# Two of four dense gate blocks scattered into the DRAM matrix by adding transfers instead of one-hot products

## The chip, the cores and the metric

The kernel runs on one core of one Trainium2 chip. The metric is the device time in microseconds (us) of one execution; for before it is the median of three runs. "Faster" and "slower" below refer to that time.

## The reference, cut to what matters

One encoder block: a shared input projection feeds an SSD mixer and an HGRN2 mixer, an output projection follows, and then a PEER layer retrieves experts. The PEER layer is what changes hands here:

```python
q = (xt @ w_query).reshape(t, PEER_HEADS, 2, PEER_HALF)
s = jnp.einsum('thpd,hpnd->thpn', q, sub_keys)
s_top, i_top = lax.top_k(s, PEER_TOPK)
...
c_top, c_idx = lax.top_k(cand, PEER_TOPK)
expert = idx1 * PEER_KEYS + idx2
gate = jax.nn.softmax(c_top, axis=-1)
...
u = u_table[eb]
hid = gelu(einsum('td,thkd->thk', xb, u)) * gb
out = einsum('thk,thkd->td', hid, v_table[eb])
```

There are 1024 tokens, 8 heads, 16 experts per head and 16384 = 128 x 128 experts of width 1024, all in float32.

## The kernel before

Tokens stand in 8 blocks of 128. The program is a row of stages with a barrier of all engines between them: `input_norm`, `ssd`, `hgrn`, `mix_out`, `peer`.

**Two ways through the experts.** Token blocks 4 to 7 are handled by gathers: one row of `u_rows` and of `v_rows` per token, head and choice. Blocks 0 to 3 (512 tokens) are handled densely: every expert's product with every one of these tokens is computed, and multiplied by a gate matrix that is zero except where the token chose the expert. That matrix is `sel` in DRAM, 8 batches of 128 x 128 x 64 float32 (64 tokens each, 4.19 MB a batch), read back in the main loop by ACT's queue (`load_sel`).

**Routing.** A unit is one token block and one head. Matrix products (`query`, `score`) make the scores; then VectorE finds the 16 experts (`route_keys`, `route_pairs`, `route_experts`) and their gates (`route_gates`, for unit n inside the route of unit n + 1). The 32 units of blocks 0 to 3 are routed in `mix_out`, which also computes the output projection block by block; a list `HEADS_IN` names for each block b the up to three heads whose query, score and two routes go with it. Heads 0 to 7 of that list are the units 0 to 15 (blocks 0 and 1), and the three heads of an entry go through TensorE in an order written out by hand at the end of `mix_out`'s tensor part. GpSimd only scales Y there.

**Building `sel` (first part of `peer`, before the main loop).** For 128 groups of 4 tokens: VectorE compares a counter with the second and the first key (`hot_b`, `hot_a`, two operations of 128x512, L1815); GpSimd multiplies `hot_b` by the gate (L1535); TensorE multiplies `hot_a` by `hot_b` for each of the 4 tokens (L1620), which gives that token's 128 x 128 gates; ACT copies them to a stage in two halves (L1696, L1699); SP stores a stage of 2.1 MB when 16 groups have filled it (L1515). `hot_a`, `hot_b` and the result bank are double-buffered by `j % 2`: VectorE starts group j when the products of j - 2 are done. Two units of block 4 and 5 are routed on the way (`ROUTE_AT`), since the gathers of the main loop need them. The main loop starts when the last stage has landed.

**Start of `hgrn`.** ACT first copies a projection that an earlier stage left in Y (`first_out`, L786), then the gates, exponentials and weights of head 0 are made by ACT and VectorE in turn; TensorE begins with L763.

The loop that feeds TensorE in the building of `sel` is, word for word:

```python
                pe.wait_ge(hot_a_ready, j + 1)
                pe.wait_ge(hot_b_ready, j + 1)
                need(pe, staged, 2 * (j - 1))
                for q in range(4):
                    mm = nc.tensor.matmul(ps_o[:, j % 2, q * P:(q + 1) * P], hot_a[j % 2][:, q, :], hot_b[j % 2][:, q, :],
                                          start=True, stop=True)
```

## Time and profile before

| | |
|---|---|
| median of 3 runs | 3931.82 us (3931.11 to 3934.82) |
| the profiled execution's own time | 3927.97 us |
| its span, first to last instruction | 3926.2 us |
| PE busy | 3574.7 us (91%) |
| DVE busy | 2930.6 us (75%) |
| POOL busy | 1394.0 us (36%) |
| ACT busy | 1015.8 us (26%) |
| mean granted TensorE clock | 0.954 |

PE is TensorE (PEld its weight loads), DVE is VectorE, ACT is ScalarE, POOL is GpSimd, SP is the engine that only issues transfers; a "q" behind a name is that engine's sequencer or queue. A share of busy time is a mean over stages that have different limits, so the prediction reads the stages one by one. Times of rows are microseconds from the first instruction of the span; L with a number is a line of the kernel before.

### The profile page before, as it was taken

The page shows a single profiled execution, that of the slowest core. Times are in us where ns is not written, and L with a number is a line of the kernel's source. Part 1 is how long each engine was busy: PE and PEld are TensorE (multiplying, and loading weights), DVE is VectorE, ACT ScalarE, POOL GpSimd, SP SyncE. Part 2 cuts the span into 40 slices and gives each one's busy share as a digit, 9 for nine tenths or more (in the row PEclk, how much of TensorE's full clock was granted, in tenths as well). Part 3 has the DMA queues.
Part 4 walks back from the last instruction along what each step waited for, and adds up shares of the span by engine and source line. Part 5 has one row for each costly group of instructions (what it writes and reads, how often), then busy time and mean ns, then how long its engine had stood idle before and what let it go on. Part 6 is the DMA issues. An engine that isn't in the chain of part 4 may idle for free.

```text
span 3926.2 us, 40482 instructions
## 1 busy us (share of the span) xinstructions
PE 3574.7 (91%) x12044; PEld 2076.7 (53%) x12044; DVE 2930.6 (75%) x6550; ACT 1015.8 (26%) x2525; POOL 1394.0 (36%) x1230
## 2 busy tenths in 40 slices
PE   7999979999979889556789999999999999999997
PEld 4666757777755556455434444444444444444443
DVE  1566767777750888788498788878889888887887
ACT  3333344444432222222211111111112111111111
POOL 1000000000010000366565555555556556555564
PEclk9999989999969999788999999999999999999999
DMA  3010000010021111123699999999999999999997
GB/s 108 28 32 27 1 22 27 27 32 21 21 101 38 72 60 59 73 86 129 256 351 378 372 360 358 353 378 365 353 363 383 377 372 364 356 363 377 363 367 278
DMA packets 294368, 829.59 MB, mean 211 GB/s; under 512 B 22448, under 2 KB 130096, under 8 KB 283952
## 3 DMA queue, kind: packets, MB, share of 16 engines
q0 software_dynamic: 147456, 536.94, 36.5%
q1 hardware_dynamic: 77008, 236.36, 15.8%
q10 hardware_dynamic: 69728, 54.27, 4.3%
q8 instruction: 71, 1.16, 0.1%
q14 instruction: 105, 0.86, 0.1%
HBM read 789.73 MB, written 37.75 MB: 211 GB/s over the span
## 4 chain that ended last, share of the span: by engine, by line
PE 43%; DMA 9%; issue 4%; DVE 3%; ACT 0%; SPq 0%; POOL 0%; DVEq 0%; ACTq 0%
PE peer_ps_o L1653 22%; PE peer_ps_d L1639 14%; DMA route_ut<-in_u_cols 6%; PE peer_ps_o L1620 4%; DMA peer_mt<-sel 3%; PE peer_ps_q L1574 3%; DVE Y L1851 1%; DVE peer_mt L1815 0%; DVE peer_ur L1840 0%; DMA sel<-peer_ur 0%; PE peer_ps_s L1583 0%; DVE Y L1868 0%; DVE route_hit L1068 0%; DVE peer_chosen L1070 0%; PE peer_ps_t L1594 0%
## 5 line engine op out<-in xcount | busy, mean ns | idle before, releaser
L1639 PE MATMUL peer_ps_d<-hnT,route_ut 128*128 128x512 f32 x2048 | 911.9, 603 | 57.2 <-DMA route_ut<-in_u_cols 56.5
L1542 POOL DMA_INDIRECT peer_ur<-in_u_rows,peer_index x512 | 590.7, 1154 | 673.5 <-DVE peer_ur L1840 551.1
L1639 PEld LDWEIGHTS peer_ps_d<-hnT,route_ut 128*128 128x128 f32 x2048 | 389.0, 193 | 560.4 <-issue 454.7
L1851 DVE SCALAR_TENSOR_TENSOR Y<-peer_vr,peer_hid,Y 128x1024 f32<-128x1024 f32 x512 | 657.3, 1284 | 8.0 <-DMA peer_vr<-in_v_rows,peer_index 7.8
L1840 DVE SCALAR_TENSOR_TENSOR peer_ur<-peer_ur,Y 128x1024 f32<-128x1024 f32 x512 | 626.2, 1223 | 31.5 <-DMA peer_ur<-in_u_rows,peer_index 31.5
L1549 POOL DMA_INDIRECT peer_vr<-in_v_rows,peer_index x512 | 561.6, 1097 | 163.8 <-issue 155.3
L1653 PE MATMUL peer_ps_o<-hnT,Y 128*128 128x512 f32 x1024 | 465.3, 596 | 23.4 <-DVE Y L1827 22.5
L1653 PE MATMUL peer_ps_o<-peer_va,Y 128*128 128x512 f32 x1024 | 466.2, 598 | 0.0
L1535 POOL TENSOR_TENSOR peer_mt<-peer_mt,peer_pickedT 128x512 f32<-128x512 f32 x128 | 181.8, 1420 | 552.4 <-DVE peer_mt L1815 552.4
L1653 PEld LDWEIGHTS peer_ps_o<-hnT,Y 128*128 128x128 f32 x1024 | 194.6, 191 | 271.3 <-issue 242.2
L1653 PEld LDWEIGHTS peer_ps_o<-peer_va,Y 128*128 128x128 f32 x1024 | 196.9, 193 | 248.1 <-issue 247.8
L1827 DVE TENSOR_TENSOR Y<-Y,peer_mt 128x512 f32<-128x512 f32 x128 | 89.0, 695 | 278.1 <-ACT Y L1707 161.2
L1620 PE MATMUL peer_ps_o<-peer_mt 128*128 128x128 f32 x1024 | 177.1, 327 | 105.0 <-issue 74.5
L1707 ACT ACTIVATE Y<-peer_ps_d 128x512 f32<-128x512 f32 x128 | 76.4, 597 | 725.0 <-PE peer_ps_d L1639 687.0
L1815 DVE TENSOR_TENSOR peer_mt<-route_count,peer_pickedT 128x512 f32<-128x512 f32 x256 | 215.5, 884 | 62.6 <-PE peer_ps_o L1620 55.2
L1714 ACT ACTIVATE peer_act_out<-peer_dots 128x2 f32<-128x2 f32 x256 | 51.2, 200 | 757.9 <-DVE peer_ur L1840 665.2
L375 PE MATMUL ssd_ps_piece<-hnT,w_group 128*128 128x512 f32 x512 | 226.7, 596 | 6.9 <-ACT ssd_raw L459 5.1
L1331 POOL IOTA mo_count_u<- 128x128 uint32 x1 | 0.2, 234 | 641.5 <-POOLq L655 641.5
L1204 PE MATMUL mo_ps_h<-mo_w,mo_yT 128*128 128x512 f32 x512 | 224.0, 596 | 1.1 <-DVE Y L1374 1.1
L1620 PEld LDWEIGHTS peer_ps_o<-peer_mt 128*128 128x128 f32 x1024 | 154.3, 231 | 128.0 <-DVE peer_mt L1815 105.9
L744 PE MATMUL hg_ps_piece<-hnT,hg_w 128*128 128x512 f32 x448 | 199.2, 598 | 0.0
L748 PE MATMUL hg_ps_piece<-hg_w,hnT 128*128 128x256 f32 x896 | 198.0, 379 | 0.0
(262 smaller groups left out, 4681.7 us busy)
## 6 DMA issues: line engine op xcount, KB each, us to landing
route_ut<-in_u_cols SPq DMA_DIRECT2D x128, 512.0 KB
peer_va<-in_v_rows SPq DMA_DIRECT2D x16, 2048.0 KB
hnT<-in_v_rows SPq DMA_DIRECT2D x16, 2048.0 KB
peer_mt<-sel ACTq DMA_DIRECT2D x64, 512.0 KB
route_wk<-in_w_route ACTq DMA_DIRECT2D x14, 1152.0 KB
route_wk<-in_w_route SPq DMA_DIRECT2D x10, 1152.0 KB
hnT<-in_w_route SPq DMA_DIRECT2D x8, 1152.0 KB, 5.1
w_group<-in_w_ssd SPq DMA_DIRECT2D x16, 512.0 KB, 4.1
```

The source lines that it names most:

```text
L375: mm = nc.tensor.matmul(bank, w[:, k, i * P:(i + 1) * P], hnT[:, half, k, :], start=(k == 0), stop=(k == KT - 1))
L744: mm = nc.tensor.matmul(bank, w[:, kt, p * P:(p + 1) * P], hnT[:, half, kt, :], start=(kt == 0), stop=(kt == KT - 1))
L748: mm = nc.tensor.matmul(bank[:, 0:2 * P], hnT[:, half, kt, cols(p - 2)], w[:, kt, 2 * P:4 * P], start=(kt == 0), stop=(kt == KT - 1))
L1204: mm = nc.tensor.matmul(ps_h[:, half, :], yT[:, k, :], w[:, k, half * 512:(half + 1) * 512], start=(k == 0), stop=(k == MT - 1))
L1542: pool.indirect_dma_start(ur[:, r % RING, :], None, u_rows, bass.IndirectOffsetOnAxis(ap=index[:, r // TOPK % 4, r % TOPK:r % TOPK + 1], a ...
L1549: pool.indirect_dma_start(vr[:, r % RING, :], None, v_rows, bass.IndirectOffsetOnAxis(ap=index[:, r // TOPK % 4, r % TOPK:r % TOPK + 1], a ...
L1620: mm = nc.tensor.matmul(ps_o[:, j % 2, q * P:(q + 1) * P], hot_a[j % 2][:, q, :], hot_b[j % 2][:, q, :], start=True, stop=True)
L1639: mm = nc.tensor.matmul(ps_d[:, e % 2, :], ut[:, e % 2, k, :], xT[:, k, :], start=(k == 0), stop=(k == KT - 1))
L1653: mm = nc.tensor.matmul(ps_o[:, o % OB, :], ht(e, tb), v_tile(e, half), start=(j == 0), stop=(j == GE - 1))
L1815: nc.vector.tensor_tensor(hot[j % 2], R.count[:].unsqueeze(1).to_broadcast([P, 4, KEYS]), pickedT[:, b % 2, part, t:t + 4].unsqueeze(2).to ...
L1840: nc.vector.scalar_tensor_tensor(out=ur[:, s, :], in0=ur[:, s, :], scalar=1.0, in1=Y[:, b, D:MIX], op0=ALU.mult, op1=ALU.mult, accum_out=d ...
L1851: nc.vector.scalar_tensor_tensor(out=hb, in0=vr[:, s, :], scalar=hid[:, c:c + 1], in1=hb, op0=ALU.mult, op1=ALU.add).then_inc(comb_done, 1)
```

## The change

With `MB` = 2, only the blocks 2 and 3 are still built by one-hot products: 64 groups instead of 128. For the blocks 0 and 1 (units 0 to 15, `SU` = 16):

- In `hgrn`, GpSimd clears a tile of 128x512, and ACT issues four transfers that write this tile over the first four batches of `sel` (16.8 MB of zeros), ahead of its first copy. GpSimd waits at the end of the stage until they have landed.
- In `mix_out`, VectorE turns each chosen expert into an address of `sel` (one operation of 128x16 more per unit, and the reduction before it now waited for). GpSimd issues for each unit 16 indirect transfers, 256 in all; each takes one gate per partition (128 numbers of 4 bytes) and adds it in DRAM at 128 addresses. It runs at most two units ahead of what has landed, and waits for the last before the stage ends.
- In `mix_out` the score of an entry's first head is moved ahead of the query of its second.
- In the groups that stay, GpSimd's multiplication is gone: VectorE makes `hot_a` first (128x512) and then `hot_b` with four `tensor_scalar` of 128x128 that compare with the key and multiply by the gate, both scalars per partition.
- The two late transposes of picks (`LATE_PICKS`) are gone, and the two routes are at groups 16 and 40.

```diff
@@ -57,6 +57,8 @@
 SELB = 64
+SU = DU // 2
+MB = DB // 2
 LOW = -3.0e38
@@ -690,6 +692,7 @@
         state = sb("state", [P, P])
+        zero = sb("zero", [P, 512])
@@ -730,6 +734,11 @@
                                  ).then_inc(w_in[i], 16)
+
+        @block.gpsimd
+        def _(pool):
+            nc.gpsimd.memset(zero[:], 0.0).then_inc(zero_ready, 1)
+            pool.wait_ge(sel_zeroed, 16 * 2 * MB)
@@ -840,6 +849,10 @@
+            act.wait_ge(zero_ready, 1)
+            for batch in range(2 * MB):
+                act.dma_start(sel[batch].rearrange("a i t -> a (i t)").rearrange("a (r c) -> a r c", c=512),
+                              zero[:].unsqueeze(1).to_broadcast([P, KEYS * SELB // 512, 512])).then_inc(sel_zeroed, 16)
             for p in range(HG_PIECES):
@@ -999,6 +1012,7 @@
             sem("best_ready"), sem("gates_ready"), sem("routed"), sem("gated"))
+        self.scattered = [sem("scattered0"), sem("scattered1")]
@@ -1123,6 +1137,10 @@
         count_u = sb("count_u", [P, KEYS], U32)
+        base_u = sb("base_u", [P, MB], U32)
+        base = sb("base", [P, MB])
+        chosen = sb("chosen", [P, TOPK])
+        sel_index = sb("sel_index", [P, SU, TOPK], U32)
         ps_y = psum("ps_y", [P, 4, P])
@@ -1245,11 +1263,10 @@
                     turn_y(b + 1, LATE)
-                if len(now) == 3:
-                    query(now[1])
                 if now:
                     score(now[0])
                 if len(now) == 3:
+                    query(now[1])
                     query(now[2])
@@ -1328,13 +1345,29 @@
         def _(pool):
-            nc.gpsimd.iota(count_u[:], pattern=[[1, KEYS]], base=0, channel_multiplier=0).then_inc(counted, 1)
+            nc.gpsimd.iota(count_u[:], pattern=[[1, KEYS]], base=0, channel_multiplier=0)
+            nc.gpsimd.iota(base_u[:], pattern=[[0, MB]], base=0, channel_multiplier=1).then_inc(counted, 1)
             pool.wait_ge(inverse, past(2))
             for b in range(NB):
                 hb = Y[:, b, D:MIX].rearrange("p (h d) -> p h d", h=HEADS)
                 nc.gpsimd.tensor_tensor(hb, hb, osq[:, b, :].unsqueeze(2).to_broadcast([P, HEADS, P]),
                                         ALU.mult).then_inc(ys_copied, 1)
 
+            pool.wait_ge(sel_zeroed, 16 * 2 * MB)
+            for n in range(SU):
+                pool.wait_ge(R.routed, n + 1)
+                pool.wait_ge(R.gated, n + 1)
+                if n >= 2:
+                    pool.wait_ge(R.scattered[n % 2], 16 * TOPK * (n // 2))
+                for k in range(TOPK):
+                    at = unit_block(n) * P + unit_head(n) * TOPK + k
+                    pool.indirect_dma_start(sel.rearrange("q a i (t o) -> (q a i t) o", o=1),
+                                            bass.IndirectOffsetOnAxis(ap=sel_index[:, n, k:k + 1], axis=0),
+                                            R.picks[D_GATE][:, at:at + 1], None,
+                                            compute_op=ALU.add).then_inc(R.scattered[n % 2], 16)
+            for i in range(2):
+                pool.wait_ge(R.scattered[i], 16 * TOPK * (SU // 2))
+
         @block.vector
@@ -1355,7 +1388,13 @@
                 route_pairs(nc, dve, own, R, n)
-                route_experts(nc, dve, own, R, n, R.picks[D_CHOSEN][:, pick_place(n)]).then_inc(R.routed, 1)
+                if n < SU:
+                    own.now(route_experts(nc, dve, own, R, n, chosen[:]))
+                    b = unit_block(n)
+                    nc.vector.tensor_scalar(sel_index[:, n, :], chosen[:], float(SELB), base[:, b:b + 1],
+                                            ALU.mult, ALU.add).then_inc(R.routed, 1)
+                else:
+                    route_experts(nc, dve, own, R, n, R.picks[D_CHOSEN][:, pick_place(n)]).then_inc(R.routed, 1)
@@ -1367,6 +1406,10 @@
             own.now(nc.vector.tensor_copy(R.count[:], count_u[:]))
+            own.now(nc.vector.tensor_copy(base[:], base_u[:]))
+            own.now(nc.vector.tensor_scalar(base[SELB:P, :], base[SELB:P, :], float(KEYS * KEYS * SELB - SELB), None,
+                                            ALU.add))
+            own.now(nc.vector.tensor_scalar(base[:, 1:2], base[:, 1:2], float(2 * KEYS * KEYS * SELB), None, ALU.add))
             for b in range(NB):
@@ -1479,11 +1521,10 @@
-        M_GROUPS = DB * P // 4
+        M_GROUPS = MB * P // 4
         PER_BATCH = SELB // 4
-        HALVES = 2 * DB * P // SELB
-        LATE_PICKS = {40: 2, 72: 3}
-        QUERY_AT, ROUTE_AT = 4, (24, 72)
+        HALVES = 2 * MB * P // SELB
+        QUERY_AT, ROUTE_AT = 4, (16, 40)
         END = PAIRS
@@ -1511,9 +1552,9 @@
                 sp.wait_ge(staged, 2 * (PER_BATCH * (batch + 1) - 1) + hh + 1)
-                to = sel[batch, :, hh * 64:(hh + 1) * 64, :]
+                to = sel[2 * MB + batch, :, hh * 64:(hh + 1) * 64, :]
                 sp.dma_start(to.rearrange("a (g i) t -> a g (i t)", g=4), stage[x % 4]).then_inc(sel_out[x % 4], 16)
-            sp.wait_ge(pick_turned, DB)
+            sp.wait_ge(pick_turned, MB)
             for e in range(2):
@@ -1529,13 +1570,6 @@
         def _(pool):
-            for j in range(M_GROUPS):
-                b, t = j // (P // 4), j % (P // 4) * 4
-                pool.wait_ge(hot_b_found, j + 1)
-                nc.gpsimd.tensor_tensor(hot_b[j % 2], hot_b[j % 2],
-                                        pickedT[:, b % 2, 2, t:t + 4].unsqueeze(2).to_broadcast([P, 4, KEYS]),
-                                        ALU.mult).then_inc(hot_b_ready, 1)
-
             def u_row(r):
@@ -1599,7 +1633,7 @@
                 for i, part in enumerate((D_FIRST, D_SECOND, D_GATE)):
-                    mm = nc.tensor.transpose(ps_t[:, i, :], picks[part][:, cols(b)], C["ident"][:])
+                    mm = nc.tensor.transpose(ps_t[:, i, :], picks[part][:, cols(DB - MB + b)], C["ident"][:])
                 mm.then_inc(pick_turned, 1)
@@ -1607,8 +1641,6 @@
             for j in range(M_GROUPS):
-                if j in LATE_PICKS:
-                    turn_picks(LATE_PICKS[j])
                 if j == QUERY_AT:
@@ -1750,8 +1781,6 @@
             for j in range(M_GROUPS):
-                if j in LATE_PICKS:
-                    pick_copy(LATE_PICKS[j])
                 if j == QUERY_AT:
@@ -1811,10 +1840,13 @@
                 t = j % (P // 4) * 4
-                for hot, part, found in ((hot_b, 1, hot_b_found), (hot_a, 0, hot_a_ready)):
-                    nc.vector.tensor_tensor(hot[j % 2], R.count[:].unsqueeze(1).to_broadcast([P, 4, KEYS]),
-                                            pickedT[:, b % 2, part, t:t + 4].unsqueeze(2).to_broadcast([P, 4, KEYS]),
-                                            ALU.is_equal).then_inc(found, 1)
+                nc.vector.tensor_tensor(hot_a[j % 2], R.count[:].unsqueeze(1).to_broadcast([P, 4, KEYS]),
+                                        pickedT[:, b, 0, t:t + 4].unsqueeze(2).to_broadcast([P, 4, KEYS]),
+                                        ALU.is_equal).then_inc(hot_a_ready, 1)
+                for q in range(4):
+                    ins = nc.vector.tensor_scalar(hot_b[j % 2][:, q, :], R.count[:], pickedT[:, b, 1, t + q:t + q + 1],
+                                                  pickedT[:, b, 2, t + q:t + q + 1], ALU.is_equal, ALU.mult)
+                ins.then_inc(hot_b_ready, 1)
@@ -1868,10 +1900,13 @@
-            own.now(nc.vector.tensor_scalar(first_key[:], picks[D_CHOSEN], 1.0 / KEYS, 0.5 / KEYS - 0.5, ALU.mult, ALU.add))
-            own.now(nc.vector.tensor_copy(picks[D_FIRST], first_key[:]))
-            nc.vector.scalar_tensor_tensor(out=picks[D_SECOND], in0=picks[D_FIRST], scalar=-float(KEYS),
-                                           in1=picks[D_CHOSEN], op0=ALU.mult, op1=ALU.add).then_inc(split_done, 1)
+            late = slice((DB - MB) * P, DB * P)
+            own.now(nc.vector.tensor_scalar(first_key[:], picks[D_CHOSEN][:, late], 1.0 / KEYS, 0.5 / KEYS - 0.5,
+                                            ALU.mult, ALU.add))
+            own.now(nc.vector.tensor_copy(picks[D_FIRST][:, late], first_key[:]))
+            nc.vector.scalar_tensor_tensor(out=picks[D_SECOND][:, late], in0=picks[D_FIRST][:, late], scalar=-float(KEYS),
+                                           in1=picks[D_CHOSEN][:, late], op0=ALU.mult, op1=ALU.add
+                                           ).then_inc(split_done, 1)
             for j in range(M_GROUPS):
```

Where instructions moved, first on ACT at the start of `hgrn` (hg_zero is the cleared tile, Y holds the projection that was left there). Before:

```order
L468 ACTIVATE Y<-ssd_ps_piece 128x256 x2
L262 UNCONDITIONAL_BRANCH
L782 UNCONDITIONAL_BRANCH
L786 ACTIVATE hg_raw_q<-Y 128x512
L786 ACTIVATE hg_raw_f<-Y 128x512
L786 ACTIVATE hg_raw_vg<-Y 128x256 x4
```

and now:

```order
L264 UNCONDITIONAL_BRANCH
L791 UNCONDITIONAL_BRANCH
L854 DMA sel<-hg_zero 2048x1x512 x4
L795 ACTIVATE hg_raw_q<-Y 128x512
L795 ACTIVATE hg_raw_f<-Y 128x512
L795 ACTIVATE hg_raw_vg<-Y 128x256 x4
```

The four clearing transfers are issued before the first copy that VectorE and TensorE wait for.

On GpSimd through `mix_out` and into `peer` (mo_sel_index are the addresses, route_ut holds the gates). Before:

```order
L1331 IOTA mo_count_u 128x128
L1335 TENSOR_TENSOR Y<-Y,osq 128x1024 x8
L1103 UNCONDITIONAL_BRANCH
L1530 UNCONDITIONAL_BRANCH
L1535 TENSOR_TENSOR peer_mt<-peer_mt,peer_pickedT 128x512 x128
L1542 DMA peer_ur<-in_u_rows,peer_index 128x1024 x5
```

and now:

```order
L1348 IOTA mo_count_u 128x128
L1349 IOTA mo_base_u 128x2
L1353 TENSOR_TENSOR Y<-Y,osq 128x1024 x8
L1364 DMA sel<-route_ut,mo_sel_index 8388608x1 x256
L1117 UNCONDITIONAL_BRANCH
L1571 UNCONDITIONAL_BRANCH
L1576 DMA peer_ur<-in_u_rows,peer_index 128x1024 x5
```

The 128 multiplications behind the barrier are gone, and 256 transfers stand before it.

On TensorE in `mix_out` at block 2 (mo_ps_q is a query, mo_ps_s a score, mo_ps_h the output projection). Before:

```order
L1204 MATMUL mo_ps_h<-mo_w,mo_yT 128x512 x16
L1186 MATMUL mo_ps_y<-ident,Y 128x128 x8
L1215 MATMUL mo_ps_q<-hnT,route_wk 128x256 x16
L1226 MATMUL mo_ps_s<-hnT,route_qs 128x128 x4
L1215 MATMUL mo_ps_q<-hnT 128x256 x16
```

and now:

```order
L1222 MATMUL mo_ps_h<-mo_w,mo_yT 128x512 x16
L1204 MATMUL mo_ps_y<-ident,Y 128x128 x8
L1244 MATMUL mo_ps_s<-hnT,route_qs 128x128 x4
L1233 MATMUL mo_ps_q<-hnT,route_wk 128x256 x16
L1233 MATMUL mo_ps_q<-hnT 128x256 x16
```

The first head's score no longer stands behind the 16 products of the second head's query.

## Rows read from the trace of the kernel before

**Rows 1.** Chain of work that ended last, shares of the span by line.

```profile
by line: PE peer_ps_o L1653 22.0%; PE peer_ps_d L1639 14.0%; DMA route_ut<-in_u_cols 5.8%; PE peer_ps_o L1620 4.1%; issue 3.7%; DMA peer_mt<-sel 2.9%; PE peer_ps_q L1574 2.6%; DVE Y L1851 0.6%; DVE peer_mt L1815 0.4%; DVE peer_ur L1840 0.3%
```

**Rows 2.** Busy time by stretch: start of hgrn, routing in mix_out, building of sel.

```profile
core 0: us, PE busy (x) PEld busy (x) DVE busy (x) ACT busy (x) POOL busy (x), PEclk, DMA share, GB/s
526.00:557.00 31.00, 5.82 (x31) 5.32 (x30) 17.58 (x44) 17.75 (x33) 0.00 (x0) 0.58 0.22 68
1264.00:1609.00 345.00, 283.89 (x1021) 187.93 (x1019) 287.75 (x1244) 74.67 (x202) 0.00 (x0) 0.91 0.16 56
1617.00:1910.00 293.00, 186.75 (x1075) 162.37 (x1074) 232.53 (x334) 87.99 (x266) 181.77 (x128) 0.84 0.25 105
```

**Rows 3.** Timeline of one group of the building of sel, engine by engine.

```profile
1706.35 1.86 DVE L1815 TENSOR_TENSOR peer_mt<-route_count,peer_pickedT 128x512 f32<-128x512 f32 x2 [0.19 <-PE peer_ps_o L1620]
...
1705.64 1.42 POOL L1535 TENSOR_TENSOR peer_mt<-peer_mt,peer_pickedT 128x512 f32<-128x512 f32 x1 [0.62 <-DVE peer_mt L1815]
1707.68 1.42 POOL L1535 TENSOR_TENSOR peer_mt<-peer_mt,peer_pickedT 128x512 f32<-128x512 f32 x1 [0.62 <-DVE peer_mt L1815]
...
1707.16 1.13 PE L1620 MATMUL peer_ps_o<-peer_mt 128*128 128x128 f32 x8 [0.92 <-issue]
```

**Rows 4.** Timeline: comparisons beside an idle POOL; products at the lower clock; a query.

```profile
1901.88 1.29 DVE L1815 TENSOR_TENSOR peer_mt<-route_count,peer_pickedT 128x512 f32<-128x512 f32 x2 [1.02 <-PE peer_ps_o L1620]
...
1620.30 4.10 PE L1620 MATMUL peer_ps_o<-peer_mt 128*128 128x128 f32 x16 [1.35 <-POOL peer_mt L1535]
...
1627.78 7.07 PE L1574 MATMUL peer_ps_q<-peer_xg,route_wk 128*128 128x256 f32 x32
```

**Rows 5.** VectorE's scalar operations: groups by form; L1343 also by ns min/median/max.

```profile
L894 DVE TENSOR_SCALAR hg_G<-hg_G,hg_oml,hg_lb 128x512 f32<-128x512 f32 x16 | 8.7, 546 | 93.5 <-ACT hg_G L804 93.5
...
L1076 DVE TENSOR_SCALAR peer_gate<-route_gx,route_gsum 128x16 f32<-128x16 f32 x32 | 7.5, 234 | 1.1
L1343 DVE TENSOR_SCALAR Y<-Y,ysq 128x1024 f32<-128x1024 f32 x8 | 7.5, 951 | 0.0
...
L1343 DVE TENSOR_SCALAR Y<-Y,ysq x8: 744/744/2389, 1158.1 to 1466.0; 128x1024 f32<-128x1024 f32 x8
```

**Rows 6.** Timeline of ACT and TensorE at the start of hgrn.

```profile
531.55 0.63 ACT L786 ACTIVATE hg_raw_q<-Y 128x512 f32<-128x512 f32 x1 [4.51 <-PEq L262]
...
553.55 3.22 PE L763 MATMUL hg_ps_att<-hg_W 128*128 128x64 f32 x14 [25.18 <-DVE hg_qs L916]
```

**Rows 7.** SP's queue in the timeline; DMA busy tenths of 0 to 40 us.

```profile
5.98 12.24 SPq L194 DMA_DIRECT2D w_group<-in_w_ssd  x5
...
6.68 4.88 SPq L194 DMA_DIRECT2D w_group<-in_w_ssd  x1
...
DMA  0389899999999999999999930000010496899710
...
1153.90 1.86 SPq L1164 DMA_DIRECT2D mo_w<-in_w_out  x4
```

**Rows 8.** Timeline: last two stores of sel, and the gather that waits for them.

```profile
1909.84 0.37 SPq L1515 DMA_DIRECT2D sel<-Y  x1
...
1910.26 1.05 SPq L1515 DMA_DIRECT2D sel<-peer_ur  x1
...
1922.61 1.16 POOL L1542 DMA_INDIRECT peer_ur<-in_u_rows,peer_index  x1 [14.44 <-DMA sel<-peer_ur]
```

**Rows 9.** GpSimd's indirect transfers: by line (min/median/max), the group, the timeline.

```profile
L1549 POOL DMA_INDIRECT peer_vr<-in_v_rows,peer_index x512: 933/937/1959, 1929.0 to 3896.6; - x171
...
L1549 POOL DMA_INDIRECT peer_vr<-in_v_rows,peer_index x512 | 561.6, 1097 | 163.8 <-issue 155.3
...
1929.04 0.94 POOL L1549 DMA_INDIRECT peer_vr<-in_v_rows,peer_index  x1 [0.31 <-issue]
```

**Rows 10.** Timeline of VectorE in mix_out: first and second route, last gate.

```profile
1275.13 0.49 DVE L1021 MAX8 route_ti<-route_sc 128x8 f32<-128x128 f32 x2 [7.35 <-ACT route_sc L1281]
1282.83 1.05 DVE L1070 TENSOR_REDUCE route_ut<-route_hit 128x16 f32<-128x864 f32 x1
...
1287.46 0.23 DVE L1076 TENSOR_SCALAR route_ut<-route_gx,route_gsum 128x16 f32<-128x16 f32 x1
1291.90 1.05 DVE L1070 TENSOR_REDUCE route_ut<-route_hit 128x16 f32<-128x864 f32 x1
...
1608.70 0.23 DVE L1076 TENSOR_SCALAR route_ut<-route_gx,route_gsum 128x16 f32<-128x16 f32 x1
```

**Rows 11.** VectorE's waits in mix_out, 1264 to 1609: total us, times, longest.

```profile
DVE route_ti L1021 <- ACT route_sc L1281: 31.0, 6, 7.3
```

More of the change, by code:

```diff
@@ L645, in _, with hgrn @@
             groups(dve, body)
-def hgrn(nc, w_hg, lb_logits, C, hnT, Y, osq, ysq):
+def hgrn(nc, w_hg, lb_logits, C, hnT, Y, osq, ysq, sel, sel_zeroed):
     with ExitStack() as ctx:
@@ L1682, in pick_copy @@
                 act.wait_ge(pick_turned, b + 1)
-                need(act, sel_made, (b - 1) * (P // 4))
-                nc.scalar.activation(pickedT[:, b % 2], ps_t[:, 0:3, :], ACT.Copy).then_inc(pick_out, 1)
+                nc.scalar.activation(pickedT[:, b], ps_t[:, 0:3, :], ACT.Copy).then_inc(pick_out, 1)
             def place_out(j, hh):
```

15 lines of the change are left out of this document (8 added, 7 removed).

## Prediction

> **What bounds the kernel now.** I read the chain of waits first, for where time counts at all, then the stretches, then timelines inside the three stretches that the change touches. The chain lies for most of its length in the main loop of `peer` [rows 1], which the change leaves as it is; from it I take only that the building of `sel` (L1620, 4.1%) is on the path too. The stages are parted by barriers, so each stretch saved or lost counts in full, and three need a sum.
>
> In the building of `sel`, 1617 to 1910, no engine is full: 293 us hold 233 us of DVE, 187 of PE, 182 of POOL [rows 2]. It is a loop over two buffers. A group repeats every 2.04 us (POOL's starts 1705.64 and 1707.68), made of POOL's 1.42 us and 0.62 us in which POOL waits for DVE, which waits for PE [rows 3]. While POOL works, DVE's pair of comparisons takes 1.86 us; beside an idle POOL 1.29 us [rows 3, 4]. In the routing part of `mix_out`, DVE is busy 288 of 345 us and sets the end, and POOL does nothing [rows 2]. At the start of `hgrn`, PE waits 25 us for a chain of ACT and DVE that begins with ACT's copy at 531.55 [rows 6].
>
> **Part 1: 64 groups instead of 128, and another inside.** Before, 293 us hold two routes of about 9.1 us each (from 1282.83 to 1291.90 is one route [rows 10]), some 9 us for a query (7.07 [rows 4]) and the first filling, and the rest, 266 us, is 128 x 2.08. Now DVE makes 1 comparison of 128x512 and 4 `tensor_scalar` of 128x128. Two comparisons end after 1.29 us and one takes 0.68, so one costs 0.61 in a row. The `tensor_scalar` with two scalars per partition is not there at 128 columns. At 512 it is 0.546 us; with one such scalar it is 0.234 at 16 columns and 0.744 at 1024 [rows 5], a slope of 0.51 ns a column. The lower bound is 0.16 (0.234 less the 0.08 by which neighbours overlap, as in the comparisons), the upper 0.46 (0.546 less the same). Between them I take 0.27: 0.234 plus 112 columns is 0.29, a second scalar adds 0.06 (0.546 against 0.485 by that line at 512), and the overlap takes 0.08 off. DVE's group is then 0.61 + 4 x 0.27 = 1.69 us. PE needs 1.13 us for the group at the upper clock and 2.05 us at the lower (16 rows in 4.10) [rows 3, 4]. The granted clock is 0.84 here [rows 2], that is 2.4 GHz for about 68% of the time and 1.2 for the rest. So a group is 0.68 x 1.69 + 0.32 x 2.05 = 1.80 us, and 64 are 115. With two routes (18) and the 9 us it comes to 142: **-151 us**. Bounds: 1.25 us a group (0.61 + 4 x 0.16) would make it -186, 2.45 us (0.61 + 4 x 0.46) -109. ACT's copies, the late transposes and the smaller split operations cost nothing: ACT is busy 88 us of 293 [rows 2], and the split stands beside the transposes of x. The last store lands 12 us after its issue as before [rows 8].
>
> **Part 2: clearing, in front of ACT's first copy.** 4 transfers of 4.19 MB in runs of 2 KB: 2048 runs each, 128 for each of the 16 DMA engines. The question is whether the issue holds ACT. In SP's queue five loads were issued back to back behind 4 MB of x, and the issue took 12.24 us, one of them 4.88; traffic goes on until about 23 us, 5 us after the last issue at 18.2 [rows 7]. Each of these loads is 1024 runs, 64 per engine; what was left after the last issue was at most two loads, 128 runs per engine. I read this as a queue that takes some 128 runs per engine and then holds its issuer. Four clearing transfers have 512, so ACT is released when three are nearly written: 12.6 MB. Two stores of `sel`, 4.19 MB, took 12.4 us from first issue to the gather behind them (1909.84 to 1922.2 or so) [rows 8], 340 GB/s, so 12.6 MB take 31 to 37 us; the 2 MB of weights for head 1, issued at the same time by SP, share this (up to 6). The clearing of the tile, 0.5 us, comes first. PE starts that much later: **+40 us**. Bounds: 2 us if the issue doesn't hold ACT, 54 if all must be written and the weights as well. POOL's wait for them at the end of `hgrn` is 550 us later and costs nothing.
>
> **Part 3: 256 adding transfers on POOL before the barrier.** Their price isn't in the trace; the nearest is the gather with 128 addresses. It is 0.94 us and 0.30 us of issue, 1.24 in a row, at the median; the mean of 512 is 1.10 + 0.30 = 1.40, the longest 1.96 + 0.30 = 2.26 [rows 9]. A gather moves 4 KB per address and an adding transfer 4 bytes; I take POOL's share to go by the number of addresses, which is the same. The two engines do get in each other's way: L1343 is 0.744 us at the median and 2.389 beside POOL's work at the stage's start [rows 5]. DVE's operations in `mix_out` are mostly under 0.3 us, as the 9 us route of some forty operations shows [rows 10], so I take 1.30 us, nearer the median than the mean, bounds 1.24 and 2.26. 256 x 1.30 = 333 us. The Trainium skill, SBUF — State Buffer, Who interferes with whom, has DVE operations in the two-port mode (`tensor_scalar`, copies) shut POOL's descriptor generation out for their whole length; by it alone the mean of the main loop would hold, 1.40, and this part be +34 and the sum -77.
>
> They can start when unit 0 has its gates: 1287.7 before [rows 10]. The moved score saves most of DVE's 7.35 us wait [rows 10] (about 5, since ACT still has to square the block first), and the two added operations take 0.3: 1283. POOL is then never short of work, since a unit takes it 20.8 us and DVE needs 9. It ends at 1283 + 333, and 2 us for the last to land: 1618, where the stage ended at 1609. DVE and PE end earlier: the six waits for scores, 31 us [rows 11], shrink to some 8, against 16 x 0.4 us of added operations, so they would be ready near 1592 and wait for POOL. **+9 us**; 1.24 gives -7, 2.26 gives +255. DVE's own savings thus bring nothing unless POOL is quick.
>
> **Sum.** -151 + 40 + 9 = -102 against the profiled execution: 3927.97 - 102 = 3826. The median of the runs shown stands 3.85 above that execution: **3830 us**.
>
> **Rival A: an adding transfer costs POOL or the DMA engines more than a gather, and the stage waits for it (slower).** An addition must read its destination too, which could double what POOL prepares: 2 x 0.94 + 0.30 = 2.18 us, and 256 of them are 558, an end at 1843, +234. The sum is then -151 + 40 + 234 = +123, 4055 us. It decides from 256c = 435 on, c = 1.70 us. For it: nothing in the trace adds in DRAM, and the issue per unit has 20 us of work against DVE's 9. Against it: the gather's price is nearly flat from its minimum to its median, and its transfers of 512 KB are far larger. Chance 0.25. (The Trainium skill, Collectives: The Full Stack, The bandwidth ceiling, says a reduce by DMA emits two read descriptors per chunk and gets half the rate of a copy; no row here shows it.)
>
> **Rival B: the issue of the clearing doesn't hold ACT.** Part 2 is +2, the sum -140: 3792 us. For it: four loads of 2 MB go out in 1.86 us elsewhere in SP's queue [rows 7], but in longer runs. Against: the 12.24 us for five loads. Chance 0.14.
>
> **Rival C: the small scalar operations are dear.** At 0.46 each, a group is 2.45 us, and part 1 gives -109: 3872 us. Chance 0.08. **Rival D: it cancels.** c between 1.67 and 1.73 leaves the time within 0.2%, some 8 us, about what a measurement of this kernel can tell from no change. Chance 0.03.
>
> **How the numbers follow.** The forecast, with c from 1.24 to 1.65 and a held ACT, has 0.50. Faster takes it, B and C: 0.72. Same 0.03, slower 0.25. The range goes from 3775, B with c = 1.24, up into A: to 3985, where c is 1.92 and some half of A's chance lies beyond; with a little below 3775, for cheap scalars, under 0.2 is left out. The forecast's own range is 3790 to 3910.
>
> **What would show each step.** Part 1: a stretch of 142 us from the first group to the last, DVE the busiest, 1.7 us a group at the upper clock. Part 2: the four DMA rows on ACT's queue some 38 us long in sum, and L763's successor starting near 593. Part 3: starts of POOL's adding transfers 1.3 us apart, without gaps, from about 1323 to 1656 with part 2's delay; DVE idle at the stage's end. The prediction is wrong if these starts lie more than 1.7 us apart, if ACT's first copy stands directly behind the issues, or if the main loop, 1922 to the end before, changes its length by more than 10 us.

## The result, and the profile after

The changed kernel takes **3969.8 us** (median of 4 runs, 3964.8 to 3975.51) against 3933.32 us for the kernel before beside it (3931.11 to 3938.25): ratio 1.0091, 95% interval 1.0074 to 1.0109. It is slower by 0.9% where 3830 us was forecast; 3969.8 lies inside the range, near its upper end. Its profiled execution took 3967.64 us with a span of 3965.9 us, 40 us more than before in both.

The chain of waits of the changed kernel, shares of the span by line, answers to [rows 1]:

```profile
by line: PE peer_ps_o L1685 21.6%; PE peer_ps_d L1671 14.0%; DMA route_ut<-in_u_cols 6.0%; DMA peer_mt<-sel 3.3%; PE peer_ps_q L1608 2.6%; issue 1.4%; PE peer_ps_o L1652 0.9%; DVE peer_mt L1847 0.9%; DVE Y L1883 0.6%; DVE peer_mt L1843 0.6%
```

The products of the one-hot groups (L1652, L1620 before) fell from 4.1% to 0.9% of the chain, and the main loop kept its shares. Where the time went shows only when the stages are laid side by side. The windows of busy time, start of `hgrn`, routing in `mix_out`, what is left of that stage, building of `sel` (columns as in [rows 2]):

```profile
526.00:588.00 62.00, 5.13 (x28) 4.61 (x28) 17.58 (x44) 17.75 (x33) 0.53 (x1) 0.55 0.81 305
1295.00:1629.00 334.00, 276.46 (x1014) 182.74 (x1012) 296.98 (x1260) 74.40 (x202) 267.25 (x162) 0.91 0.35 58
1629.00:1807.00 178.00, 0.00 (x0) 0.00 (x0) 0.00 (x0) 0.00 (x0) 145.79 (x95) 0.50 0.22 0
1816.00:1949.00 133.00, 85.00 (x555) 74.08 (x555) 121.92 (x398) 44.68 (x136) 0.00 (x0) 0.90 0.26 104
```

The third row is the answer: for 178 us nothing works but POOL. The granted TensorE clock is 0.50 there, that is 1.2 GHz, with PE doing nothing. In the first row the same work of ACT and DVE as before (17.75 and 17.58 us) takes twice the stretch. The last row is the saving, 133 us where [rows 2] had 293.

The timelines of the changed kernel, first ACT at the start of `hgrn` (start, duration, engine, line; in brackets the idle time before and what ended it):

```profile
532.33 31.14 ACTq L854 DMA_DIRECT2D sel<-hg_zero  x4
563.52 0.63 ACT L795 ACTIVATE hg_raw_q<-Y 128x512 f32<-128x512 f32 x1 [36.23 <-issue]
...
585.48 3.22 PE L772 MATMUL hg_ps_att<-hg_W 128*128 128x64 f32 x14 [56.87 <-DVE hg_qs L929]
```

The four clearing transfers hold ACT's queue for 31.14 us, and PE begins at 585.48 instead of 553.55 [rows 6]: 32 us. Next, POOL's adding transfers in the timeline: the first ones, the last one, and the first gather behind them:

```profile
1312.70 1.80 POOL L1364 DMA_INDIRECT sel<-route_ut,mo_sel_index  x1 [108.61 <-DVE route_ut L1090]
1314.80 1.68 POOL L1364 DMA_INDIRECT sel<-route_ut,mo_sel_index  x1 [0.30 <-issue]
...
1801.88 1.55 POOL L1364 DMA_INDIRECT sel<-route_ut,mo_sel_index  x1 [0.30 <-issue]
1962.45 1.01 POOL L1576 DMA_INDIRECT peer_ur<-in_u_rows,peer_index  x1 [159.01 <-DMA sel<-peer_ur]
```

The same transfers by line (min/median/max in ns, first and last start):

```profile
L1364 POOL DMA_INDIRECT sel<-route_ut,mo_sel_index x256: 1548/1551/2439, 1312.7 to 1801.9; - x128
```

They start where the prediction had them, 1312.7 for 1283 plus the delay of the clearing, and run without gaps; but an adding transfer takes 1.55 us and 0.30 of issue where the gather's row has 0.94 and 0.30. From the first start to the last is 489.2 us, 1.92 us each. The other engines at the end of the stage, last gate and next stage:

```profile
1627.59 0.23 DVE L1090 TENSOR_SCALAR route_ut<-route_gx,route_gsum 128x16 f32<-128x16 f32 x1
1807.54 0.29 DVE L1904 TENSOR_SCALAR peer_first_key<-route_ut 128x256 uint32<-128x256 f32 x1 [179.72 <-PEq L1117]
...
1807.54 1.09 PE L1628 MATMUL peer_ps_t<-ident,Y 128*128 128x128 f32 x4 [207.23 <-PEq L1117]
```

The waits of DVE in that stage, total us, times, longest, answer to [rows 11]:

```profile
DVE route_ti L1035 <- ACT route_sc L1298: 11.6, 6, 2.5
```

DVE's wait for scores fell from 31.0 to 11.6 us, and with 31 us of delay from the clearing its last gate is ready at 1627.8. The gain can't show in the time, since POOL is done 176 us later. The building of `sel`, one group after another on DVE:

```profile
1821.96 0.69 DVE L1843 TENSOR_TENSOR peer_mt<-route_count,peer_pickedT 128x512 f32<-128x512 f32 x1
1822.57 1.11 DVE L1847 TENSOR_SCALAR peer_mt<-route_count,peer_pickedT 128x128 f32<-128x128 f32 x4
1823.60 0.68 DVE L1843 TENSOR_TENSOR peer_mt<-route_count,peer_pickedT 128x512 f32<-128x512 f32 x1
```

and the scalar operations by line:

```profile
L1847 DVE TENSOR_SCALAR peer_mt<-route_count,peer_pickedT x256: 332/339/347, 1816.8 to 1946.9; 128x128 f32<-128x128 f32 x128
```

A group is 1.64 us (1821.96 to 1823.60): 0.61 for the comparison and 1.03 for the four scalar operations. The balance, as lengths before and after, from the starts of the stages: up to the start of `mix_out` +30, from the clearing; `mix_out` 457 and 625 us, **+168**; from its end to the first gather 313.4 and 155.0, **-158**; the main loop 2003.6 and 2003.4, nothing. That is +40.

### The profile page after: what moved, and what is told of

It is laid out like the page before. It is cut to its first block, busy times and chain, and to the rows that moved or that the text cites. A ratio compares the mean times of both kernels' runs of the same rounds, so it can differ in the third digit from the quotient of the medians.

```text
span 3965.9 us, 39408 instructions
## 1 busy us (share of the span) xinstructions
PE 3464.7 (87%) x11526; PEld 1981.2 (50%) x11526; DVE 2832.3 (71%) x6633; ACT 972.8 (25%) x2395; POOL 1621.5 (41%) x1360
## 4 chain that ended last, share of the span: by engine, by line
PE 40%; DMA 10%; DVE 4%; issue 1%; ACT 0%; SPq 0%; DVEq 0%; ACTq 0%
PE peer_ps_o L1685 22%; PE peer_ps_d L1671 14%; DMA route_ut<-in_u_cols 6%; DMA peer_mt<-sel 3%; PE peer_ps_q L1608 3%; PE peer_ps_o L1652 1%; DVE peer_mt L1847 1%; DVE Y L1883 1%; DVE peer_mt L1843 1%; DMA sel<-peer_ur 0%; DVE peer_ur L1872 0%; PE peer_ps_s L1617 0%; DVE Y L1900 0%; DVE route_hit L1082 0%; DVE peer_chosen L1084 0%
## 5 line engine op out<-in xcount | busy, mean ns | idle before, releaser
L1364 POOL DMA_INDIRECT sel<-route_ut,mo_sel_index x256 | 413.0, 1613 | 186.3 <-DVE route_ut L1090 108.9
L359 POOL TENSOR_TENSOR ssd_awide<-ssd_a,ones 128x512 f32<-128x512 f32 x32 | 33.8, 1055 | 449.9 <-PE ssd_ps_rows L422 402.8
L757 PEld LDWEIGHTS hg_ps_piece<-hg_w,hnT 128*128 128x128 f32 x896 | 168.1, 190 | 21.7
```

The costliest lines, as they stand in the source:

```text
L757: mm = nc.tensor.matmul(bank[:, 0:2 * P], hnT[:, half, kt, cols(p - 2)], w[:, kt, 2 * P:4 * P], start=(kt == 0), stop=(kt == KT - 1))
L1364: pool.indirect_dma_start(sel.rearrange("q a i (t o) -> (q a i t) o", o=1), bass.IndirectOffsetOnAxis(ap=sel_index[:, n, k:k + 1], axis=0) ...
```

## The experiments

The theory after this result (A): the addition itself makes each transfer dearer on GpSimd, by about 0.6 us, and the stage waits for the last of 256. The rivals: (B) any transfer of 4-byte pieces costs this, with or without the addition; (C) the DMA engines are what is slow, since each addition must read; (D) DVE's work beside it slows POOL. (These letters are apart from those of the prediction's rivals.) The clearing, the groups and the moved score are tried apart from it.

### The addition taken away

```diff
-                                            R.picks[D_GATE][:, at:at + 1], None,
-                                            compute_op=ALU.add).then_inc(R.scattered[n % 2], 16)
+                                            R.picks[D_GATE][:, at:at + 1], None).then_inc(R.scattered[n % 2], 16)
```

> The changed kernel with the 256 transfers as plain scatters (no addition in DRAM; the matrix is cleared, so they write the same gates). Theory A (the addition is what makes a transfer take GpSimd 1.55 us where a gather takes 0.94): the instruction falls to about 0.94, the spacing from 1.91 to 1.25-1.3 us, and the projection stage ends some 160 us earlier, near 3805-3820 us in all. Theory B (the addition costs GpSimd nothing; the direction or the 4-byte elements do): 1.55 us and 3965-3970 us as with the addition.

It does not write quite the same gates: where two heads of a token chose the same expert, the addition sums their gates and a plain transfer keeps one. That is what the addition is for; this kernel leaves it out.

The profiled execution took 3996.44 us, longer than with the addition, and still its transfers are short, by line:

```profile
L1364 POOL DMA_INDIRECT sel<-route_ut,mo_sel_index x256: 955/962/1844, 1315.3 to 1696.1; - x128
```

962 ns at the median against 1551, so B falls for the duration. The whole time can't be read from this execution. In its windows DVE is busy 8.87 us between 1350 and 1400, where the changed kernel has 42.59. PE and ACT stand as well, with waits that no instruction of the kernel explains, while POOL keeps its pace there (39 transfers in these 50 us). I took this for a disturbance by the recording of many small transfers and had the same kernel timed, below.

### Gathers of 4 bytes instead

Each transfer reads 4 bytes at 128 addresses of `u_rows` into SBUF; clearing and everything else as changed. The core of the edit:

```diff
-                    pool.indirect_dma_start(sel.rearrange("q a i (t o) -> (q a i t) o", o=1),
-                                            bass.IndirectOffsetOnAxis(ap=sel_index[:, n, k:k + 1], axis=0),
-                                            R.picks[D_GATE][:, at:at + 1], None,
-                                            compute_op=ALU.add).then_inc(R.scattered[n % 2], 16)
+                    pool.indirect_dma_start(dump[:, n * TOPK + k:n * TOPK + k + 1], None,
+                                            u_rows.rearrange("e (d o) -> (e d) o", o=1),
+                                            bass.IndirectOffsetOnAxis(ap=sel_index[:, n, k:k + 1], axis=0)
+                                            ).then_inc(R.scattered[n % 2], 16)
```

> The changed kernel with 256 gathers of one 4-byte number per partition from the table u_rows, with the same addresses, in place of the adding transfers (the gates of blocks 0 and 1 are left out, so two blocks get no expert output). If elements of 4 bytes or an address list over 4-byte rows cost GpSimd the extra 0.6 us: 1.55 us each and about 3965 us. If scattering as such does: 0.94 us each, near 3805-3820 us.

The gathers by line:

```profile
L1365 POOL DMA_INDIRECT mo_dump<-in_u_rows,mo_sel_index x256: 942/947/1762, 1312.6 to 1692.1; - x128
```

947 ns, the duration of the gather of 4 KB rows (937 in [rows 9]). Neither the size of a piece nor the direction sets GpSimd's time; that step of the prediction holds. The profiled time, 3982.5 us, has the same standstills; this kernel has no other execution, so what it does to the whole time is not shown.

### The plain scatter, timed

The kernel of the first experiment again.

> The plain scatter again, timed. Its one execution so far was under the profiler, GpSimd's instruction was 0.96 us in place of 1.55, and yet TensorE, VectorE and ACT all stood still together for tens of us (a gather of 4 bytes in its place did the same). Theory A: that standstill belongs to the recording of so many small transfers a us, and unrecorded executions show what 256 x (1.61 - 1.00) us = 156 us less of GpSimd are worth: the stage then ends with GpSimd near 1642 in place of 1807, 3800-3815 us. Theory B: small transfers this close together really hold the engines: unrecorded executions stay near 3990 us. (Where a token's two heads chose the same expert, one of the two gates is lost in this kernel.)

**3823.15 us** (3820.68 to 3826.56), ratio 0.972 (0.9701 to 0.974): 147 us less than the changed kernel, and 8 above the end of the range expected. This time the recorded execution (span 3824.8 us) is undisturbed. By line:

```profile
L1364 POOL DMA_INDIRECT sel<-route_ut,mo_sel_index x256: 954/958/2007, 1312.2 to 1656.9; - x128
```

and in the windows of busy time, routing and the rest of the stage:

```profile
1295.00:1629.00 334.00, 276.18 (x1010) 182.22 (x1008) 294.86 (x1260) 74.13 (x202) 243.70 (x233) 0.91 0.18 58
1629.00:1662.00 33.00, 0.00 (x0) 0.00 (x0) 0.00 (x0) 0.00 (x0) 22.02 (x23) 0.50 0.02 0
```

The starts are 1.35 us apart (344.7 us for 255), and the stretch in which only POOL works shrinks from 178 to 33 us. 256 x (1.92 - 1.35) is 146 us, the whole difference of the medians. With that the forecast of 3830 us is nearly met, but in part by luck. In this kernel the clearing costs 30 us where 40 were forecast, `mix_out` is 23 us longer where 9 were, and the building saves 158 where 151 were. D accounts for little in both kernels. While DVE works, POOL's transfers take 267.25 / 162 = 1.65 us, afterwards 1.55; plain ones 1.05 (243.70 / 233) and 0.96.

### How the addition's price goes with the addresses

Two kernels with transfers of 64 addresses, with and without the addition. Both leave out the gates of half the tokens. The edit of the first; the second drops `compute_op=ALU.add` too:

```diff
-                                            bass.IndirectOffsetOnAxis(ap=sel_index[:, n, k:k + 1], axis=0),
-                                            R.picks[D_GATE][:, at:at + 1], None,
+                                            bass.IndirectOffsetOnAxis(ap=sel_index[0:SELB, n, k:k + 1], axis=0),
+                                            R.picks[D_GATE][0:SELB, at:at + 1], None,
```

> The changed kernel with each of the 256 adding transfers carrying the gates of tokens 0 to 63 alone (64 addresses instead of 128); it leaves out the gates of tokens 64 to 127 of the two scattered blocks. Clearing and products as changed. If the addition costs GpSimd by the address (0.60 us more than plain at 128 addresses), a transfer of 64 should take the plain one of 64 plus 0.30 us, and the 256 of them end some 77 us after those of the run with 64 addresses without the addition. If the addition costs a fixed time per instruction, the difference is again 0.60 us and 150 us. Under either the transfers may fall under the head rate of the stage (1.3 us a transfer), so that the whole times of the two runs come together near 3820; the durations on POOL tell the two apart.

> The same 64-address transfers without the addition; it leaves out the gates of tokens 64 to 127 and loses one gate where two heads of a token chose one expert. If a plain transfer costs GpSimd by the address, the 0.95 us at 128 addresses falls to about half with some fixed part, 0.5 to 0.6 us; if fixed per instruction it stays at 0.95. The difference to the run with the addition is 0.30 us (by address) or 0.60 us (fixed).

With the addition, by line:

```profile
L1364 POOL DMA_INDIRECT sel<-route_ut,mo_sel_index x256: 1406/1410/2442, 1315.2 to 1770.6; - x128
```

and without:

```profile
L1364 POOL DMA_INDIRECT sel<-route_ut,mo_sel_index x256: 887/892/1775, 1315.0 to 1644.9; - x128
```

1.410 and 0.892 us, where 128 addresses took 1.551 and 0.958. Halving the addresses saves 0.14 and 0.07 us. The addition's extra is 0.52 us at 64 addresses and 0.59 at 128: most of it is a fixed price of the instruction. By a straight line through the two sizes, which is an estimate, 0.44 of the 0.59 us don't go with the addresses, and 0.83 of the plain transfer's 0.958. The times are 3939.26 us (ratio 1.0014, 1.0002 to 1.0026; one of its eight executions took 14258.91 us, which nothing here explains, and is not in the ratio) and 3806.87 (two executions, 0.9677, 0.9644 to 0.9711; before 3932.23). I had expected the two to come together near 3820, because the heads would set the pace; wrong, since even at 1.29 us a transfer the last one starts at 1644.9, behind DVE's last gate at 1627.2, so all of POOL's difference stays visible.

The queue of these transfers in the pages: packets, MB, share of the 16 DMA engines. Of the changed kernel, then in one fence each of the plain scatter (timed one), of 64 addresses with the addition, and without:

```profile
q0 software_dynamic: 184320, 537.08, 38.7%
```

```profile
q0 software_dynamic: 155648, 537.08, 37.7%
```

```profile
q0 software_dynamic: 167936, 537.02, 38.2%
```

```profile
q0 software_dynamic: 155648, 537.02, 37.7%
```

The gathers of the main loop are 147456 packets in all (1024 x 144). What is above that, divided by 256, is 144 packets for an adding transfer of 128 addresses and 80 for one of 64, that is one per address and 16; for a plain one it is 32 with 128 addresses and with 64, and 32 also in the gathers of 4 bytes (155648 again). So small plain pieces are recorded in bundles and adding ones singly. The additions do cost the DMA engines more: where POOL works alone their share is 0.22 with them and 0.02 without. C falls for the time all the same. In the whole stage of the changed kernel POOL never waits for a landing, the engines' share is 0.22 to 0.35, and the first adding transfer, with none before it, already takes 1.80 us.

### The clearing issued by SP

```diff
                 sp.dma_start(w[:, :, part], w_hg[1, :, :, part]).then_inc(w_in[i], 16)
+            sp.wait_ge(zero_ready, 1)
+            for batch in range(2 * MB):
+                sp.dma_start(sel[batch].rearrange("a i t -> a (i t)").rearrange("a (r c) -> a r c", c=512),
+                             zero[:].unsqueeze(1).to_broadcast([P, KEYS * SELB // 512, 512])).then_inc(sel_zeroed, 16)
...
-            act.wait_ge(zero_ready, 1)
-            for batch in range(2 * MB):
-                act.dma_start(sel[batch].rearrange("a i t -> a (i t)").rearrange("a (r c) -> a r c", c=512),
-                              zero[:].unsqueeze(1).to_broadcast([P, KEYS * SELB // 512, 512])).then_inc(sel_zeroed, 16)
```

> The changed kernel with the four clearing transfers issued by SP behind its loads of head 1's weights, where nothing waits for SP for some 60 us, in place of by ACT ahead of its first copy. If the issue held ACT for 31 us and nothing else is lost: about 31 us less than the changed kernel, 3936-3942 us, ratio to before 1.000-1.003. If the traffic of 16.8 MB itself costs (weights late, copies slower): less than 20 us of it come back.

In its timeline, ACT's first copy and SP's queue:

```profile
535.28 0.63 ACT L799 ACTIVATE hg_raw_q<-Y 128x512 f32<-128x512 f32 x1 [4.52 <-PEq L264]
...
539.95 30.62 SPq L733 DMA_DIRECT2D sel<-hg_zero  x4
```

and by line the adding transfers:

```profile
L1364 POOL DMA_INDIRECT sel<-route_ut,mo_sel_index x256: 1548/1550/2436, 1282.3 to 1771.4; - x128
```

**3935.91 us** (3930.44 to 3948.8; before 3933.06), ratio 1.0005 (0.9989 to 1.0021): no difference that can be measured to the kernel before, and 34 us less than the changed one. The same four transfers hold SP for 30.6 us, and there nobody waits for it. POOL's first transfer moves from 1312.7 to 1282.3, and its duration stays as it was. Together with the plain scatter:

> Plain scatter and the clearing issued by SP. Theory A: 31 to 34 us less than the plain scatter with ACT's clearing, 3768-3782 us, since GpSimd's last transfer still ends behind VectorE. Theory B: near 3955 us.

**3788.24 us** (3785.34 to 3796.82), ratio 0.9641 (0.9617 to 0.9664); starts from 1282.2 to 1625.6. That is 35 us below the plain scatter with the clearing on ACT, so the two costs add up. The time is above the expected 3768 to 3782, because the plain scatter itself was.

### The parts that gain, without the scatter

The kernel before with DVE making `hot_b` by four `tensor_scalar`, all 128 groups, GpSimd's multiplication gone (the part of the edit on DVE):

```diff
-                for hot, part, found in ((hot_b, 1, hot_b_found), (hot_a, 0, hot_a_ready)):
-                    nc.vector.tensor_tensor(hot[j % 2], R.count[:].unsqueeze(1).to_broadcast([P, 4, KEYS]),
-                                            pickedT[:, b % 2, part, t:t + 4].unsqueeze(2).to_broadcast([P, 4, KEYS]),
-                                            ALU.is_equal).then_inc(found, 1)
+                nc.vector.tensor_tensor(hot_a[j % 2], R.count[:].unsqueeze(1).to_broadcast([P, 4, KEYS]),
+                                        pickedT[:, b % 2, 0, t:t + 4].unsqueeze(2).to_broadcast([P, 4, KEYS]),
+                                        ALU.is_equal).then_inc(hot_a_ready, 1)
+                for q in range(4):
+                    ins = nc.vector.tensor_scalar(hot_b[j % 2][:, q, :], R.count[:], pickedT[:, b % 2, 1, t + q:t + q + 1],
+                                                  pickedT[:, b % 2, 2, t + q:t + q + 1], ALU.is_equal, ALU.mult)
+                ins.then_inc(hot_b_ready, 1)
```

> The kernel before with one part of the change: GpSimd's multiplication is gone and VectorE makes hot_b with four scalar operations, for all 128 groups; no scattering, no clearing, scores in the old order. If the groups of the changed kernel (64 in 133 us with two routes) carry over: 133 + 64 x 1.72 = 243 us where it was 293, so 50 us less, 3880-3888 us. Rival: a part of the gain came from fewer stores; then under 35 us.

In the windows of busy time, the building of `sel`:

```profile
1617.00:1858.00 241.00, 160.61 (x1080) 138.52 (x1078) 226.45 (x718) 88.63 (x267) 0.00 (x0) 0.94 0.31 128
```

**3873.3 us** (3871.12 to 3877.96), ratio 0.9846 (0.9832 to 0.986). The stretch of 293 us in [rows 2] is 241 now, with DVE busy 226 of it: DVE alone sets the pace, and the mean clock rose from 0.84 to 0.94. The medians differ by 62 us, the two recorded executions by 56; 50 were expected. The kernel before with the score order alone:

```diff
-                if len(now) == 3:
-                    query(now[1])
                 if now:
                     score(now[0])
                 if len(now) == 3:
+                    query(now[1])
                     query(now[2])
```

> The kernel before with the score of an entry's first head ahead of the query of its second, nothing else. VectorE waited 31.0 us for scores before and 11.6 after; if it sets the stage's end, 15-19 us less: 3914-3918 us. Rival: TensorE or the loads of routing weights take over and less than 8 us come.

Among DVE's waits in `mix_out`:

```profile
DVE route_ti L1021 <- ACT route_sc L1280: 11.6, 6, 2.5
```

**3912.41 us** (3906.31 to 3917.53), ratio 0.9941 (0.9927 to 0.9955), 23 us less, where 15 to 19 were expected; the waits fell by 19.4. In the changed kernel, whose stage ends with POOL, the same edit can bring nothing. Both together:

> Both parts together on the kernel before. The stages are parted by a barrier, so the gains add: 65-70 us less, 3864-3868 us.

**3856.27 us** (3850.49 to 3863.21), ratio 0.9799 (0.9783 to 0.9815): 79 us less than the 3935.4 of before, near the sum of the two alone (62 and 23), and more than the 65 to 70 expected. Two small parts of the change, without a single transfer, leave the changed kernel 114 us behind.

### One block scattered instead of two

If the price of an adding transfer can't be changed, their number can. Block 0 alone is scattered, 128 transfers; a unit's transfers now start when the last unit's have landed; the blocks 1 to 3 are built in 96 groups; SP clears two batches. The core of the edit, on top of the clearing by SP:

```diff
-SU = DU // 2
-MB = DB // 2
+SU = DU // 2
+MB = 3
+ZB = 2 * (DB - MB)
...
-            for n in range(SU):
+            for n in range(0, SU, 2):
...
-                if n >= 2:
-                    pool.wait_ge(R.scattered[n % 2], 16 * TOPK * (n // 2))
+                if n >= 2:
+                    pool.wait_ge(R.scattered[0], 16 * TOPK * (n // 2))
```

> Only block 0 is scattered (128 adding transfers, each unit's wait for the unit before it), blocks 1 to 3 are built by one-hot products (96 groups), and the clearing of 8.4 MB is issued by SP. Theory: the changed kernel loses because 256 transfers of 1.91 us (490 us) don't fit into the 320 us that VectorE needs after the first unit; 128 do (245 us and 8 gaps of some 4 us). Then the projection stage ends with VectorE, some 11 us earlier than before, the building takes 133 + 32 x 1.72 = 188 us where it took 293, and the whole is 3933 - 105 - 11 = 3817 us. Rival: GpSimd's transfers slow VectorE down or something else in the stage holds it; then it is above 3850 us.

The adding transfers by line:

```profile
L1365 POOL DMA_INDIRECT sel<-route_ut,mo_sel_index x128: 1547/1551/2419, 1282.9 to 1564.2; - x128
```

In the windows of busy time, the routing and the building of `sel`:

```profile
1264.00:1594.00 330.00, 274.52 (x1020) 181.27 (x1018) 293.83 (x1253) 74.46 (x202) 211.98 (x128) 0.93 0.31 59
1603.00:1787.00 184.00, 121.44 (x814) 105.26 (x813) 173.72 (x558) 65.44 (x198) 0.00 (x0) 0.93 0.29 121
```

and the first gather in the timeline:

```profile
1800.14 1.00 POOL L1576 DMA_INDIRECT peer_ur<-in_u_rows,peer_index  x1 [234.40 <-DMA sel<-peer_ur]
```

**3810.19 us** (3809.28 to 3818.41), ratio 0.9679 (0.9658 to 0.9701): it computes all of the reference, beats both kernels, and is 160 us below the changed one. Of its 123 us against the kernel before, the two small parts bring 79 without any transfer; the scattered block itself is worth the 46 us between 3856.27 and this. The last transfer starts at 1564.2, and DVE's last gate at 1593.4 ends the stage, so that the transfers are wholly hidden and the saved waits for scores count. The building takes 184 us; (184 - 27) / 96 is 1.64 us a group, as in the changed kernel.

## Why the prediction was wrong

**The failing step** is the choice in Part 3: "I take POOL's share to go by the number of addresses, which is the same", with c = 1.30 us from the gather. The experiments bear out a price near that for a transfer that does not add (1.35 us between starts of the plain scatter), and the 4-byte gather shows that bytes don't count. "By the number of addresses" is wrong too, since 64 addresses cost 0.892 us and 128 cost 0.958; it did no harm, the number being the same. But the addition adds 0.59 us to POOL's own duration, and 1.92 is above the 1.70 where I had put the break-even and the sign of being wrong. With 1.92 in its formula, 1283 + 492 + 2 - 1609 makes this part +168 instead of +9; measured +168. The whole sum would then have been 3989 us; the 19 us to the measured 3969.8 are mostly the clearing and the building, both forecast too dear. That the measured time lies inside the range is no credit to the forecast: that part of the range belonged to rival A. (Two bounds there are a little off: 1.92 gives 3988 and not 3985, and 1.65 gives 3919 and not 3910.) The row of the gather could not show this: it holds no addition.

**Rival A** (slower, 4055 us) had the mechanism and the place: an adding transfer costs POOL more than a gather, and the stage waits for it. Its size was a guess of doubled preparation, 2.18 us; the runs show 1.92. The break-even was right and cheap to state, and with a price known only from an operation that does not add, 0.25 was too little for everything beyond it. The Trainium skill (Collectives: The Full Stack, The bandwidth ceiling) has a reduce by DMA emit two read descriptors per chunk at half the rate of a copy. That is a rule on the engines' rate, which bounds nothing here, so no run tests its factor. An adding transfer has 144 recorded packets, as many as the gather, and on GpSimd 1.6 times the plain one's duration.

**Part 1** (-151) was right: -158. The scalar operation costs 0.26 in a row (1.03 / 4) for 0.27. Of the 142 us forecast for the stretch 9 were not needed: I had mixed in groups at the lower clock by the old stretch's 0.84, and the granted clock was 0.90, with a group at 1.64 us instead of 1.80.

**Part 2** (+40) was right in kind, and its term some 10 too large. ACT is held, for 31.14 us and not 38. ACT's queue (q10) and SP's (q1, the weights) moved this, packets and MB, from 530 us to ACT's release at 563.46:

```profile
q10 hardware_dynamic: 4717, 9.60, 75.0%
q1 hardware_dynamic: 3264, 2.11, 19.5%
```

and behind the release, from 563.46 to 600:

```profile
q10 hardware_dynamic: 3539, 7.18, 50.4%
```

So the weights did share the time, as allowed for. But the queue let ACT go when 9.60 MB of zeros were out and not 12.6: 3539 packets, 221 per engine, were still to come, where I had read 128 from [rows 7]. And the engines moved 384 GB/s (windows from 533 to 563.46), not 340. **Rival B** of the prediction falls by the same 31.14 us, **rival C** by the 0.26 us, and **rival D**, a chance of 0.03, did not come.

**The rest of the stage.** "DVE's own savings thus bring nothing unless POOL is quick" held: the moved score saved 23 us alone, and here POOL ends 176 us behind DVE. "Start at 1283, no gaps, two units ahead never binding" held too. The main loop's length did not change, as forecast. The rule on DVE's two-port mode (the Trainium skill, SBUF — State Buffer, Who interferes with whom) was to give 1.40 us a transfer; the plain scatter has 1.35 over all and about 0.1 us more beside a working DVE than beside an idle one, so the measured price lies midway between the rule's and the 1.30 I took, and the slowing beside DVE is there but small.

Left open is what GpSimd does in the extra 0.59 us. The runs show that it is mostly fixed per instruction and that the pieces are no longer bundled; whether the one causes the other was not tried. Nor was a transfer that carries several addresses per partition, which the fixed price speaks for.

## What to carry to other kernels

Price an indirect transfer by the instruction, and take that price from one with the same options: an option that looks free in the code, here the addition, took 1.92 us from start to start in place of 1.35. When work moves to an idle engine in front of a barrier, the question is count times price against the stretch that hides it (here 310 us, from the first gates to the stage's end, enough for 128 adding transfers and not for 256); choose the count to fit, and with the clearing on SP in both, the same idea goes from no gain (ratio 1.0005) to 3.2% faster. Try the small parts of a change alone as well: two of them gave 2.0% here. Large transfers belong on the queue of an engine for which nobody waits: here the queue held its issuer until 9.60 of 16.78 MB were gone.

## What the runs showed of the hardware that was not expected

- GpSimd's duration for one indirect transfer, at the median: gather of 4 KB rows 0.94 us, of 4 bytes 0.947, plain scatter of 4 bytes 0.958, adding scatter 1.551, all with 128 addresses; with 64 addresses 0.892 and 1.410.
- Recorded packets of 4-byte transfers: 32 each when plain, whether 64 or 128 addresses; 80 and 144 when adding.
- Four transfers of 4.19 MB hold their issuing engine for 31 us, from ACT as from SP. ACT was released with 3539 packets still to come, 221 for each of the 16 DMA engines.
- The share of the DMA engines where POOL works alone is 0.22 with adding transfers and 0.02 with plain ones, though both carry the same 4-byte pieces.
- One kernel with 256 small plain scatters was recorded once with a span of 3994.7 us and once with 3824.8, while its timed runs lie between 3820.68 and 3826.56. In the first recording PE, DVE and ACT stood still for long stretches of `mix_out` while POOL went on; whether the recording did that or something else in that execution is open. A recorded execution should be held against the timed runs before its waits are explained.
